# Two-layer hybrid diffusion backbone: context rows split by ScalarE and TensorE, expert tokens dealt four to a step in the choices of experts, first row of two residuals made ahead

## The reference

```python
def peer_ffn(u, wq, k1, k2, eu, ev):
    def chunk(xc):                              # 128 tokens
        q = (xc @ wq).reshape(PEER_CHUNK, PEER_HEADS, 2, half)
        s1 = jnp.einsum('thd,hnd->thn', q[:, :, 0], k1)
        s2 = jnp.einsum('thd,hnd->thn', q[:, :, 1], k2)
        v1, i1 = lax.top_k(s1, PEER_TOPK)       # 16 of 128 keys, 8 heads
        v2, i2 = lax.top_k(s2, PEER_TOPK)
        ...                                     # 16 best of the pairs: eidx, top_s
        g = jax.nn.softmax(top_s, -1)
        h = jax.nn.gelu(jnp.einsum('thkd,td->thk', eu[eidx], xc), approximate=False)
        return jnp.einsum('thk,thkd->td', g * h, ev[eidx])
...
x = layer_norm(DEEPNORM_ALPHA * x + g2_l * ffn, ln2_g[i], ln2_b[i])
```

## Time and profile before

| | us |
|---|---|
| median of 3 runs (2982.92 to 2992.35) | 2991.45 |
| the profiled execution | 2984.76 |
| its span | 2982.9 |
| PE busy (80% of the span) | 2376.2 |
| DVE busy (63%) | 1882.3 |
| POOL busy (24%) | 726.0 |
| ACT busy (16%) | 469.6 |

### The profile page before, as it was taken

The page is one execution under the profiler, slowest core; times in us unless marked ns, Lnnn a source line. Parts: engine busy times, 40 slices in busy tenths (PEclk is TensorE's granted clock), DMA queues, the critical chain, the costliest instruction groups (busy, mean ns, idle before and its releaser), DMA issues.

```text
span 2982.9 us, 34831 instructions
## 1 busy us (share of the span) xinstructions
PE 2376.2 (80%) x11960; PEld 1316.6 (44%) x11960; DVE 1882.3 (63%) x6191; ACT 469.6 (16%) x1139; POOL 726.0 (24%) x779
## 2 busy tenths in 40 slices
PE   7989997888999778678979978887797576766565
PEld 6878894444655445124545543332696111121111
DVE  2879987776555557857854455655457855555555
ACT  3151131233010111012010012221331000000000
POOL 0000003233223222332223223332002333333332
PEclk8999997788999889568989997765898556565656
DMA  8718858998999989888999999998445999999996
GB/s 317 267 61 323 314 209 328 382 403 335 405 383 416 400 321 364 341 333 353 379 395 420 421 402 398 405 395 353 181 145 228 379 362 413 403 370 418 409 401 279
DMA packets 155376, 1029.87 MB, mean 345 GB/s; under 512 B 19136, under 2 KB 29888, under 8 KB 34496
## 3 DMA queue, kind: packets, MB, share of 16 engines
q0 software_dynamic: 110592, 805.36, 66.8%
q1 hardware_dynamic: 31648, 209.70, 18.1%
q10 hardware_dynamic: 12960, 12.59, 1.3%
HBM read 1018.66 MB, written 8.91 MB: 344 GB/s over the span
## 4 chain that ended last, share of the span: by engine, by line
PE 52%; DMA 21%; DVE 20%; issue 3%; ACT 3%; POOL 1%; ACTq 0%; SPq 0%; DVEq 0%; POOLq 0%
DMA ring<-in_peer_uv,eT 19%; PE PS L1486 13%; DVE ring L2680 8%; PE PS L996 8%; PE PS L1470 6%; PE PS L917 5%; PE PS L1108 2%; PE PS L1023 2%; PE PS L1042 2%; PE PS L919 2%; POOL ring L807 1%; PE PS L1085 1%; PE PS L1216 1%; PE PS L874 1%; PE PS L1318 1%
## 5 line engine op out<-in xcount | busy, mean ns | idle before, releaser
L2680 DVE CUSTOM_DVE_ANT_0 ring<-ring,PS 128x512 f32<-128x512 f32 x1536 | 992.9, 685 | 771.2 <-PE PS L1470 587.2
L807 POOL DMA_INDIRECT ring<-in_peer_uv,eT x768 | 724.4, 943 | 2225.6 <-PE PS L1486 1367.5
L1470 PE MATMUL PS<-xr,onesb 3*128 3x512 bf16 x1536 | 508.7, 471 | 385.3 <-DVE hcol L2680 319.8
L1486 PE MATMUL PS<-ring,zcol 128*32 128x512 f32 x3072 | 563.5, 871 | 88.0 <-DVE zcol L2690 86.5
L1470 PEld LDWEIGHTS PS<-xr,onesb 3*128 3x128 bf16 x1536 | 103.0, 95 | 898.6 <-DVE hcol L2680 481.3
L1486 PEld LDWEIGHTS PS<-ring,zcol 128*32 128x32 f32 x3072 | 101.4, 140 | 362.8 <-issue 219.8
L996 PE MATMUL PS<-uT,W 128*128 128x256 f32 x1024 | 246.4, 389 | 0.0
L1985 ACT ACTIVATE ge<-hdot 128x4 f32<-128x4 f32 x192 | 39.5, 206 | 1218.4 <-DVE hdot L2685 1218.4
L996 PEld LDWEIGHTS PS<-uT,W 128*128 128x128 f32 x1024 | 191.6, 192 | 48.2 <-issue 23.3
L2060 DVE CUSTOM_DVE_ANT_0 ring<-ring 128x1024 f32<-128x1024 f32 x160 | 190.3, 1222 | 8.2 <-DMA ring<-in_w_rows 4.1
L917 PE MATMUL PS<-uT,W 128*128 128x256 f32 (+1 forms) x672 | 157.6, 388 | 7.8 <-ACT uT L1570 7.4
(11 more groups left out here) (358 smaller groups left out, 2298.3 us busy)
## 6 DMA issues: line engine op xcount, KB each, us to landing
ring<-in_w_rows SPq DMA_DIRECT2D x40, 1024.0 KB, 8.0
W<-in_w_in SPq DMA_DIRECT2D x30, 1024.0 KB, 9.6
W<-in_w_gate SPq DMA_DIRECT2D x16, 1408.0 KB, 7.5
W<-in_w_gate SPq DMA_DIRECT2D x16, 1280.0 KB, 7.8
W<-in_w_out SPq DMA_DIRECT2D x20, 1024.0 KB, 5.0
W<-in_w_gate SPq DMA_DIRECT2D x16, 1152.0 KB, 10.4
ring<-in_w_q SPq DMA_DIRECT2D x16, 1024.0 KB, 13.5
xr<-xrows ACTq DMA_DIRECT2D x768, 6.0 KB
```

What stands on the lines that cost most here:

```text
L807: pool.indirect_dma_start(ring[:, slot, :], None, (peer_uv0, peer_uv1)[b.l], bass.IndirectOffsetOnAxis(eT[:, f % 2, t:t + 1], 0)).then_inc ...
L1470: T.matmul(bank(x_banks[i]), onesb[p0:p0 + 3, 0:1].to_broadcast([3, P]), xr[p0:p0 + 3, g % 2, h * 512:(h + 1) * 512], start=True, stop=Tru ...
L1486: last = T.matmul(PS[k * NR:(k + 1) * NR, (6 + h) * 512:(7 + h) * 512], zcol[:, g % 2, k, NR - 1 - at:2 * NR - 1 - at], ring[:, slot, D + ...
L2680: V.tensor_tensor_reduce(out=u_half, in0=u_half, in1=bank(x_banks[2 * (q * TOK + n) + h]), scale=1.0, scalar=0.0, op0=ALU.mult, op1=ALU.ad ...
```

## The change

1. `back(BC0)`: the two `rows` steps with DVE's ten operations and their waits are gone; one empty `rows` step stays. The context's rows are turned, cut and subtracted as in BL0 and BL1, by PE and ACT, in the first four of the eight steps of the choice, and stored in its steps 4 and 5.
2. Shares: `gate` becomes `own` in BL0 and BC0 (1.1 to 1.04), the choice's steps in BC0 become `pick` (2.5 to 4.0), those in BL1 `sel1` (2.5 to 4.0), `late` goes from 2.4 to 1.9 and is `late1` in BL1 (4.0).
3. The four last units get steps of their own, `fill`, with one token each, ahead of the `late` steps, where DVE has nothing but tokens.
4. The two transposes that bring the first tile's choice to ACT are made one unit later (u 9 and 10 for 8 and 9).
5. Residuals of the last tile of CTX0 and LAT1 ("awaited"): the first row is made earlier (for CTX0 at the end of `part`, for LAT1 at the end of the first tile's residual) and copied by ACT into the place of y. DVE multiplies it with banks 6 and 7 directly; ACT's copy after the last `weigh` is gone. Banks change so that this row has bank 4 to itself.

Tokens that the shares hand out in each place, counted through SCRIPT:

| place | before | after |
|---|---|---|
| BL0 fill + late | 0 + 19 | 4 + 15 |
| BC0 gates (64 steps) | 70 | 66 |
| BC0 out, sum, ln | 24 | 24 |
| BC0 rows | 5 | 1 |
| BC0 wq | 40 | 40 |
| BC0 choice (8 steps) | 20 | 32 |
| "after" between LAT0's residuals | 15 | 11 |
| BL1 fill + late | 0 + 19 | 4 + 32 |
| BL1 second choice (8 steps) | 20 | 32 |
| "after" ahead of LAT1's first residual | 95 | 66 |

```diff
-         "sum": 1.5, "rows": 2.5, "wq": 0.95, "sel": 2.5, "res": 2.0,
-         "late": 2.4, "cut": 0.8, "part": 1.2}
+         "sum": 1.5, "rows": 1.0, "wq": 0.95, "sel": 2.5, "res": 2.0,
+         "fill": 1.0, "late": 1.9, "late1": 4.0, "sel1": 4.0, "cut": 0.8, "part": 1.2, "own": 1.04, "pick": 4.0}
...
         def row_banks(f, tt):
-            return (4, 4, 4) if f == LAT1 and tt == 0 else (2, 4, 2)
+            return (4, 4, 4) if f == LAT1 and tt == 0 else (4, 2, 4) if awaited(f, tt) else (2, 4, 2)
+
+        def awaited(f, tt):
+
+            return f != LAT0 and tt == TT - 1
...
+                for u in range(16 - BEHIND, 16):
+                    unit(1, u)
+                    if u % 2 == 0:
+                        scores(1, u // 2 - 1)
+                    yield "fill"
...
+                def row_turned(tt):
+                    for k in range(KD):
+                        last = T.matmul(bank(2 + 2 * tt + k // 4, (k % 4) * P, (k % 4 + 1) * P), uT[:, k, tt * P:(tt + 1) * P], ident[:, :],
+                                        start=(k % 4 == 0), stop=False, skip_group_check=True)
+                    last.then_inc(a["urow"], 1)
+
+                def row_less(tt, part_):
+                    pe.wait_ge(a["xcut"], a.at("xcut", TT * part_ + tt + 1))
+                    for h in range(2):
+                        last = T.matmul(bank(2 + 2 * tt + h), less[:, :], xs[:, tt, part_, h * 512:(h + 1) * 512],
+                                        start=False, stop=(part_ == 1), skip_group_check=True)
+                    last.then_inc(a["xless"], 1)
+
                 for q in range(8):
+                    if q < 2:
+                        row_turned(q)
+                    if q == 1:
+                        row_less(0, 0)
+                    if q == 2:
+                        row_less(1, 0)
+                        row_less(0, 1)
+                    if q == 3:
+                        row_less(1, 1)
...
                 for q in range(8):
+                    if q == 0:
+                        row_cut(0, 0)
+                    if q == 1:
+                        row_cut(1, 0)
+                        row_cut(0, 1)
+                    if q == 2:
+                        row_cut(1, 1)
+                        row_cut(0, 2)
+                    if q == 3:
+                        row_cut(1, 2)
+                        act.wait_ge(a["xcut"], a.at("xcut", 3 * TT))
+                    if q in (4, 5):
+                        stored(b, a, q - 4)
                     if q == 7:
                         chosen(b, a, 0, 4)
-                    yield "sel"
+                    yield "pick"
...
-                for tt in range(TT):
-                    rows_ = two(2 + 2 * tt)
-                    dve.wait_ge(a["urow"], a.at("urow", tt + 1))
-                    ch.link(V.tensor_copy(xs[:, tt, 0, :], rows_))
-                    V.tensor_tensor(xtmp, rows_, xs[:, tt, 0, :], ALU.subtract).then_inc(a["xread"], 1)
-                    dve.wait_ge(a["xread"], a.at("xread", tt + 1))
-                    ch.link(V.tensor_copy(xs[:, tt, 1, :], xtmp))
-                    ch.link(V.tensor_tensor(xtmp, xtmp, xs[:, tt, 1, :], ALU.subtract))
-                    V.tensor_copy(xs[:, tt, 2, :], xtmp).then_inc(a["xsplit"], 1)
-                    dve.wait_ge(a["xsplit"], a.at("xsplit", tt + 1))
-                    yield "rows"
+                yield "rows"
...
+            def first_row(f):
+                row(4, mod[:, OF[f].l, OF[f].s, 40:48]).then_inc(at_of["residual", f]["rows2"], 1)
...
+                if awaited(f, tt):
+                    dve.wait_ge(first_row_s, q)
+                    dve.wait_ge(weighed, (q + 1) * NG)
+                    V.tensor_tensor(y_of(f, tt), two(6), y_of(f, tt), ALU.mult).then_inc(y_out, 1)
+                    dve.wait_ge(y_out, 2 * q + tt + 1)
```

More of the change, by code:

```diff
@@ L743, in early @@
                 yield from conv()
-                yield from gates()
+                yield from gates("gate")
             def back(b):
@@ L749, in back @@
                 if not b.early:
-                    yield from gates()
+                    yield from gates("own")
                 else:
@@ L1774, in apart @@
                 yield TILE_READY
-                for q in range(LATE):
-                    u = 16 - BEHIND + q
-                    if u < 16:
-                        unit(1, u)
-                    if u <= 16 and u % 2 == 0:
-                        scores(1, u // 2 - 1)
-                    yield "late"
+                for u in range(16 - BEHIND, 16):
+                    unit(1, u)
+                    if u % 2 == 0:
+                        scores(1, u // 2 - 1)
+                    yield "fill"
+                for q in range(LATE):
+                    if q == 0:
+                        scores(1, 7)
+                    yield "late1" if b.early else "late"
                 if b.early:
@@ L1871, in back, with row_cut @@
                 yield from modulate(a, l, s, uT, 24, 32)
-                for tt in range(TT):
-                    yield "rows"
+                yield "rows"
+                def row_cut(tt, part_):
+                    if part_:
+                        act.wait_ge(a["xless"], a.at("xless", TT * (part_ - 1) + tt + 1))
+                    else:
+                        act.wait_ge(a["urow"], a.at("urow", tt + 1))
+                    A(xs[:, tt, part_, :], two(2 + 2 * tt), ACT.Copy).then_inc(a["xcut"], 1)
                 for u in range(21):
@@ L1924, in part_ @@
                 kept(len(JOBS) - 1)
+                first_row(CTX0)
             def attend(a):
@@ L1965, in residual, with first_row @@
                         spread(at_of["residual", f, tt], 0, 1)
+                    if q == 2 and f == LAT1 and tt == 0:
+                        first_row(f)
                     yield "res"
+            def first_row(f):
+                a = at_of["residual", f]
+                r = at_of["residual", ORDER[ORDER.index(f) - 1]]
+                act.wait_ge(r["x_new"], r.at("x_new", TT))
+                if f == CTX0:
+                    for parity in range(2):
+                        act.wait_ge(kept_s[parity], 8 * KD)
+                act.wait_ge(a["rows2"], a.at("rows2", 4))
+                A(y_of(f, TT - 1), two(4), ACT.Copy).then_inc(first_row_s, 1)
             def x_rows(f, g):
@@ L1995, in experts @@
                                     act.wait_ge(r["x_new"], r.at("x_new", tt + 1))
-                                if f == CTX0 and tt:
-                                    for parity in range(2):
-                                        act.wait_ge(kept_s[parity], 8 * KD)
                                 A(y_of(f, tt), two(6), ACT.Copy).then_inc(y_out, 1)
@@ L2569, in apart @@
                 yield TILE_READY
+                for q in range(BEHIND):
+                    yield "fill"
                 for q in range(LATE):
```

111 lines of the change are left out of this document (53 added, 58 removed).

## The result

The changed kernel takes 2954.63 us (median of 4 runs, 2952.43 to 2957.01) beside 2988.68 us for the kernel before on the same chip: a ratio of 0.9888, 95% interval [0.9868, 0.9908]. The forecast was 2968 us, between 2944 and 2997. It is faster, as forecast, by 34 us (1.1%) where I had 23; the interval leaves no room for no change. The profiled span went from 2982.9 to 2955.2 us, 27.7 less; the sum of the prediction had 20.1.

A forecast was written before the change was run, and what follows sets the result against it. The prediction took DMA transfers as the bound, 2.55 us a token; its terms summed to -20.1 us, giving 2964.7 us by the profiled execution or 2971.4 by the median, stated as 2968, range 2944 to 2997.

The forecast's parts named there:

- BL0, first tokens: Start of BL0: one token per late unit brings units 13 and 15 forward; -2 us, bounds -3.2 and +6.
- BC0 gates: Gates of BC0: four tokens fewer at 2.55 us each, -10.2 us; only about 4 us if PE is the bound.
- BC0 rows and `wq`: DVE's row operations and their tokens go, -13 us, and the x-row wait in `wq`, -4; together -17, between -12 and -21.
- BC0 choice: CTX0's choice with 32 tokens, cuts, turns and stores takes 99.5 us in place of 65: +34.5, between +23 and +50.
- between LAT0's residuals: Four tokens fewer between LAT0's two residuals: -10.2 us, between -8 and -12.
- LAT1 start and second choice: Idle transfers at 2290 filled, -4.5 us, and those of choice and `cut` hidden by more tokens, -8.5: together -13.
- LAT1's last residual: End of kernel: DVE starts right after the last `weigh`, the first row being made earlier; -3.0 us.
- The yardstick: Tokens-only window 2412 to 2636, share 1.01 at 410 GB/s: transfers set the time, 2.55 us a token.
- The crowded choice: Slower rival: cuts and turns in CTX0's choice delay gelu, `weigh` and slots; choice over 128 us, kernel 3000 us; chance 0.13.
- The idle transfers only move: No-difference rival: idle time won returns elsewhere; only -6 us, 2979 by the profiled execution, 2985 by the median; chance 0.17.
- Much faster: Rival: idle time in the touched stretches goes but a third of BC0's; 48 us gained, 2943 us; chance 0.12.
- The signs: Expected marks: CTX0's choice near 100 us, POOL waits under 5, LAT1 share near 1, prompt last residual, 4 us longer stand.

The follow-up runs named there:

- e_dverows: Changed kernel with the context's rows cut by DVE again in two `rows` steps and stored in `wq`, the choice keeping 32 tokens: 2952.94 us, ratio 0.9883.
- b_bc0: Changed kernel with BC0's old shares back (own 1.04 to 1.1, pick 4.0 to 2.5): 2956.15 us, ratio 0.9896.
- k_bc0all: Changed kernel with BC0 wholly as before (rows cut by DVE, rows 2.5, own 1.1, pick 2.5): 2965.02 us, ratio 0.9952.
- r_lateonly: Changed kernel with only sel1 back (4.0 to 2.5), so 36 tokens before LAT1's second choice and 20 in it: 2961.03 us, ratio 0.9905.
- a_bl1: Changed kernel with BL1's old shares back (late1 4.0 to 2.4, sel1 4.0 to 2.5), `fill` kept: 2975.44 us, ratio 0.9957.
- c_never: Changed kernel with both residuals of the last tile as before, no row made ahead: 2954.84 us, ratio 0.9889.
- o_again: The changed kernel itself run once more, on the same chip as three other follow-up kernels: 2962.62 us, ratio 0.9912.

## Why the prediction was right, and where it was off

| term | predicted | by the traces |
|---|---|---|
| BL0, first tokens | -2 | 0 |
| BC0 gates | -10.2 | -12.3 |
| BC0 rows and `wq` | -17 | -18.6 - 5.6 = -24.2 |
| BC0 choice | +34.5 | +30.0 |
| between LAT0's residuals | -10.2 | -6.9 |
| CTX0's last residual | -3.0 | -2.9 |
| LAT1 start and second choice | -13 | -11.5 |
| LAT1's first residual | +3.8 | +2.9 |
| LAT1's last residual | -3.0 | -3.3 |
| sum | -20.1 | -28.2 |

The parts of BC0 go by PE's landmarks of the table above. By the windows that the forecast was made in, the choice is 100 us in place of 65, +35: the edges of a part move its term by some 5 us.

Between the terms the trace drifts (from 13.4 us at token 260 to 11.5 at 500 where nothing was changed, and 1.4 at CTX0's end), which gives the 27.7.

- **The yardstick held.** The gain came out of idle transfers: the same bytes moved at 348 GB/s in place of 344. A token costs 2.55 us in the pure stretch before and after (60 gathers in the 152 us from 2268 to 2420, 2.53).
- **BL0.** The wait for unit 15 fell (12.88 us until 484.15 before, 3.38 now), and the idle transfers of 480 to 488 are gone: the share is 1.01 from 476 to 500, though POOL stands 11.45 us for a `weigh` until 492.25 and DVE is busy 9.52 of 10 us at 476 to 486. Yet the changed kernel is 1 us behind at token 20 and level at 68. Both kernels have a further lull behind it, at 550 to 560 before (0.66) and at 530 to 540 now (0.75). So the 3.2 us were filled and nothing was won by it; why is not shown.
- **BC0 is the term that was mis-sized, -2.9 against -13.4.** Three of its four parts came out better than forecast: four tokens fewer in the gates gave 12.3 us, 3.1 each, not 2.55; rows and `wq` gave 7 us more; and the stores' wait, 5.8 us that I put back into the choice, did not come back (no wait for x rows there). The length of the choice itself was right, its composition less so: turns, cuts and stores cost 15.4 us there beside 32 tokens (e_dverows) and 3.0 beside 20 (b_bc0), where I had 6 + 5.8 for either. The sentence that read the -2.9 as "some 9 us less of the 44" of idle transfers doesn't fit its own sum: tokens and bytes of BC0 are the same in both kernels, so 2.9 us less in time are 2.9 less idle.
- **The step that failed is the adding.** I gave the rows -17 us as a gain of their own, less 6 + 5.8 for cuts and stores, -5.2 in all, and to the dealing (-10.2 in the gates, -10.2 between the residuals, +22.7 for 12 more tokens in the choice) +2.3 us, no gain. b_bc0, e_dverows and k_bc0all show that each of the two alone gives some 16 us, and both together no more: one lull of 11 to 16 us that either removes. "Nearly all of it sets the time there" was true only of the thin choice that followed; with 32 tokens in it, DVE's rows cost nothing.
- **LAT1.** The sum of -13 was nearly right, and its reason wrong in part. I put 8.5 us on the choice's tokens and thought of `late` as tokens under cover. r_lateonly shows that with 32 tokens in `late` the choice's further ones give nothing; a_bl1, with both thin, costs some 20 us. Which share `late` has alone was not run. "It now starts with slots full" did not hold in `cut`: the hand-over (11.00 us) and the x rows (14.86) are stands there as before.
- **Residuals.** Each piece has the predicted size where it arises, but without the row ahead CTX0's loss is made good by token 548 (c_never); their sum is too small to be told in the times.
- **The rivals.** The crowded choice did not come: 100 us, 28 below its point of decision. "The idle transfers only move" is right of the row split beside the dense choice, of the choice's further tokens in LAT1 and of the hand-over, and wrong of the whole. Much faster (2943) lies nearer to the time than the forecast does (11.6 and 13.4 us), so that the time alone doesn't choose between them; what it lacks is above all the 9 us of lull in LAT1's choice and `cut`, which stay, and a part of the 16 us that are still idle in BC0's `wq` and choice (7 and 9).
- **The signs.** Four of the five came (the choice of CTX0, LAT1's share of 1.01 until 2420, the last residual, the longer stand, 2.65 us of the 4). No wait of POOL for the units over 5 us holds in the first trace (4.12) and not in the second (7.84). The share in the gates did not fall with fewer tokens there (0.98 and 0.99).

## What to carry to other kernels

Where transfers set the time, list the lulls and count each once. Two edits that fill the same lull don't add, and only taking each out alone, and both together, shows it. Whether tokens pay ahead of a lull or in it has to be tried: in CTX0's choice more tokens alone took the share from 0.77 to 0.98 (e_dverows), in LAT1's they gave nothing once the steps ahead were full. And where a full ring of gathers is reached, look at what small transfers stand behind large ones in one queue: here they were the next wait.

## What the runs showed of the hardware

- Four 6 KB loads issued 2.4 us behind 768 KB of stores in the ACT queue were there for PE 19.3 us after their issue (2449.60 to 2468.89), at a share of 0.98 from 2445 to 2469. In a second trace, 2.9 us behind, it was 14.1 us. With the stores in SP's queue and a share of 0.97 and 1.00 it was 8.5 and 9.0 us.
- Two traces of the same kernel (changed and o_again) lie 5.9 us apart at the first expert group (473.7 and 479.6 us). This distance stays between 3.0 and 7.6 us up to token 512 and between 4.1 and 5.5 from 600 on, but at LAT1's start it goes to 13.4 us at token 516 and 8 at 548. So one trace tells a stage to some 2 us where the order of the engines is the same, and less around a start.
- In the gates, with PE 224 of 236 us busy and the share at 0.99, taking out four tokens saved 12.3 us, more than their transfers alone (10.2). The stage took 249.5 us in all three traces with 70 tokens and 237.2 to 237.4 in all eleven with 66.
